# Two attentions with other bank turns, one semaphore renewal fewer, and a query stage joined to its gather, in a float32 network on one core

## The reference, cut to what matters

```python
# retention, per head of 4 (256 wide for q and k, 512 wide for v)
o = (q k^T * decay) v  (+ the same through a carried state)
o = layer_norm(o);  y = (o * silu(g)) @ w_out
# forgetting attention, per head of 16 (64 wide)
p = softmax(q k^T + cum_q - cum_k, causal);  o = p v;  y = (o * silu(g)) @ w_out
# PEER, per token: 8 heads, 16 keys of each half, 16 pairs of them
s1, s2 = q1 @ keys1.T, q2 @ keys2.T
v1, i1 = top_k(s1, 16); v2, i2 = top_k(s2, 16)
vals, c = top_k(v1[:, None] + v2[None], 16)
expert = i1[c // 16] * 128 + i2[c % 16]          # 128 experts a token
act = gelu(h @ u_tab[expert].T)
out = (softmax(vals) * act) @ v_tab[expert]
```

## Time and profile before

| | |
|---|---|
| median of 3 runs | 3270.94 us (3265.91 to 3271.77) |
| profiled execution, its own time | 3268.9 us |
| its span (first to last instruction) | 3267.0 us |
| PE busy | 2811.6 us (86%) |
| DVE busy | 1836.7 us (56%) |
| POOL busy | 1197.8 us (37%) |
| ACT busy | 884.6 us (27%) |
| gathered by POOL's queue | 536.94 MB, 40.4% of 16 DMA engines' span |

### The profile page before, as it was taken

One profiled execution on the slowest core, in us unless ns is written; L12 is line 12 of the kernel. 1 busy time (PEld: TensorE's weight loads), 2 busy tenths in 40 slices (PEclk: granted clock), 3 DMA queues, 4 the chain that ended last, 5 costly groups with the idle time before them and its releaser, 6 DMA issues. The chain is left out here.

```text
span 3267.0 us, 30767 instructions
## 1 busy us (share of the span) xinstructions
PE 2811.6 (86%) x10832; PEld 1870.9 (57%) x10832; DVE 1836.7 (56%) x3274; ACT 884.6 (27%) x1621; POOL 1197.8 (37%) x1220
## 2 busy tenths in 40 slices
PE   6999899999799989889999996778677867787777
PEld 5888477875477667689877782333233323333333
DVE  4772545333453556455624368787688568854554
ACT  2122123342345646332432331111111111111111
POOL 0000000000020414145000117777777777777774
PEclk7999999999899999999999998889798988898989
DMA  6462032310123022300222439999999999999997
GB/s 218 152 219 91 13 123 74 102 52 1 39 78 103 27 66 78 122 1 1 92 90 87 152 107 388 419 416 417 419 419 419 419 418 419 419 419 419 419 419 315
DMA packets 228769, 706.45 MB, mean 216 GB/s; under 512 B 23188, under 2 KB 25492, under 8 KB 227735
## 3 DMA queue, kind: packets, MB, share of 16 engines
q0 software_dynamic: 147456, 536.94, 40.4%
q1 hardware_dynamic: 81176, 167.76, 15.0%
HBM read 694.13 MB, written 10.49 MB: 216 GB/s over the span
## 5 line engine op out<-in xcount | busy, mean ns | idle before, releaser
L3028 PE MATMUL work_banks<-v_rows,sig 128*128 128x512 f32 x1408 | 659.5, 627 | 121.9 <-ACT sig L3019 116.3
L3028 PEld LDWEIGHTS work_banks<-v_rows,sig 128*128 128x128 f32 x1408 | 280.5, 201 | 495.7 <-issue 340.0
L219 DVE TENSOR_TENSOR weights_low<-weights_raw,weights_high 128x2048 fp32r<-128x2048 f32 x108 | 251.3, 2327 | 451.0 <-ACT weights_high L214 440.8
L3028 PE MATMUL work_banks<-weights_raw,sig 128*128 128x512 f32 x512 | 284.3, 718 | 189.4 <-ACT sig L3019 189.4
L2925 DVE CUSTOM_DVE_ANT_0 proj_banks<-u_rows,work_banks 128x1024 f32<-128x1024 f32 x256 | 314.1, 1230 | 206.7 <-DMA u_rows<-in_peer_u_dram,eidx 206.7
L277 PE MATMUL proj_banks<-h_low,weights_high 128*128 128x512 f32 x896 | 358.6, 400 | 30.4 <-DVE weights_low L219 12.9
L2700 POOL DMA_INDIRECT v_rows<-in_peer_v_dram,eidx x352 | 332.2, 944 | 115.8 <-issue 91.5
L214 ACT CAST weights_high<-weights_raw 128x2048 fp32r<-128x2048 f32 x108 | 205.9, 1906 | 617.7 <-PE proj_banks L277 600.9
L277 PE MATMUL proj_banks<-h_high,weights_high 128*128 128x512 f32 x896 | 353.1, 394 | 0.0
L277 PE MATMUL proj_banks<-h_high,weights_low 128*128 128x512 f32 x896 | 353.0, 394 | 0.0
L3028 PEld LDWEIGHTS work_banks<-weights_raw,sig 128*128 128x128 f32 x512 | 116.5, 234 | 356.1 <-issue 291.3
(11 more groups left out here) (487 smaller groups left out, 4607.1 us busy)
## 6 DMA issues: line engine op xcount, KB each, us to landing
weights_raw<-in_w_in_dram SPq DMA_DIRECT2D x36, 1024.0 KB, 5.1
weights_raw<-in_ret_w_in_dram SPq DMA_DIRECT2D x24, 1024.0 KB, 5.2
ret_gate<-in_mod_w_dram SPq DMA_DIRECT2D x20, 1024.0 KB, 8.2
weights_raw<-in_fox_w_in_dram SPq DMA_DIRECT2D x16, 1024.0 KB, 5.2
weights_raw<-in_ret_w_out_dram SPq DMA_DIRECT2D x8, 1024.0 KB, 5.0
weights_raw<-in_peer_w_q_dram SPq DMA_DIRECT2D x8, 1024.0 KB, 5.2
v_rows<-in_peer_v_dram,eidx POOLq DMA_INDIRECT x352, 16.6
ret_v<-in_mod_w_dram SPq DMA_DIRECT2D x4, 1024.0 KB, 13.3
```

What stands on the lines that cost most here:

```text
L219: nc.vector.tensor_tensor(wlo[h][:, :, :], raw[h][:, :, :], whi[h][:, :, :].bitcast(F32), ALU.subtract).then_inc(w_split[h], 1)
L3028: last = nc.tensor.matmul(pa[:, half, :], diag[:, s, e, :], v_row(s, e)[:, half * CW:(half + 1) * CW], start=(first and e == 0), stop=(las ...
```

## The change

It has four parts.

1. Retention's attention: three output banks instead of two and one for transposes. A bank is free as soon as it is normalised (`nrm_ready`), the gate product goes to POOL, `nrm` has two buffers, and a tile's transposes come three tiles after its outputs.
2. Forgetting attention: DVE multiplies the outputs of the two banks into the gate first, in turn with ACT's copies of the sums so that the two engines are never on one bank, and the reciprocal follows. values(m+1) waits for the two products and the two copies (`o_read`, `sums_ready`) alone.
3. The `recycle_semaphores()` between `delta_inputs` and `delta_rule` is left out.
4. The query stage and the gather stage become one block. The gather's buffers lie over the split weights and the input parts, now with names of their own (`over_split`, `over_parts`), and waits on `first_used` and `s_full` stand in for the barrier. Four more v rows are gathered inside the query part, 16 instead of 12. PE does scores(c-1) after two of the four tiles of a first half instead of after all four. DVE takes the first top_head of a chunk before the split of the next half chunk, and `experts(0, 0)` right after the heads 2 and 3.

```diff
-                nrm = sbuf(st2, "ret_nrm", [P, CW])
+                nrm = sbuf(st2, "ret_nrm", [P, 2, CW])
+                O_BANKS, LAG = 3, 3
...
+                        def output(n):
+                            h, t = n // TT, n % TT
+                            pe.wait_ge(s_read, n + 1)
+                            if n >= O_BANKS:
+                                pe.wait_ge(nrm_ready, n - O_BANKS + 1)
...
+                        def transposes(n):
+                            h, t = n // TT, n % TT
+                            pe.wait_ge(gated, n + 1)
+                            if n:
+                                pe.wait_ge(tr_read, n)
...
+                        for n in range(RET_HEADS * TT):
+                            if n % TT == 0 and n // TT + 1 < RET_HEADS:
+                                scores(n // TT + 1)
+                            output(n)
+                            if n >= LAG:
+                                transposes(n - LAG)
...
-                                nc.vector.tensor_tensor(sg[:, t, cols], sg[:, t, cols], nrm[:, :],
-                                                        ALU.mult).then_inc(gated, 1)
...
+                            pool.wait_ge(nrm_ready, n + 1)
+                            cols = slice(h * RET_HV, (h + 1) * RET_HV)
+                            nc.gpsimd.tensor_tensor(sg[:, t, cols], sg[:, t, cols], nrm[:, n % 2, :], ALU.mult
+                                                    ).then_inc(gated, 1)
...
                                 pe.wait_ge(o_read, m)
+                                pe.wait_ge(sums_ready, 2 * m)
...
+                            act.wait_ge(down_read, m + 1)
...
+                            nc.vector.tensor_tensor(sg[down, m, :], sg[down, m, :], pa[down, 3, :], ALU.mult
+                                                    ).then_inc(down_read, 1)
+                            dve.wait_ge(sums_ready, 2 * m + 1)
+                            nc.vector.tensor_tensor(sg[up, m, :], sg[up, m, :], pa[up, 2, :], ALU.mult
+                                                    ).then_inc(o_read, 1)
...
-                            dve.wait_ge(scaled_gate, m + 1)
-                            nc.vector.tensor_tensor(sg[up, m, :], sg[up, m, :], pa[up, 2, :], ALU.mult)
-                            nc.vector.tensor_tensor(sg[down, m, :], sg[down, m, :], pa[down, 3, :], ALU.mult
-                                                    ).then_inc(o_read, 1)
...
+            over_split = sbuf(st2, "rows_over_split", [P, GE, D], side="right")
+            over_parts = sbuf(st2, "rows_over_parts", [P, GE, D], side="right")
+            vr = sbuf(st2, "v_rows", [P, 3, D])
...
+                    sp.wait_ge(s_full, 4 * n)
...
-                        project_half(pe, c, 0, parts)
+                        project_half(pe, c, 0, parts, tiles=range(0, 2))
                         scores(c - 1)
+                        project_half(pe, c, 0, parts, tiles=range(2, 4))
                         project_half(pe, c, 1, parts)
...
+                    pool.wait_ge(first_used, state["g"] + n + 1)
+                    for e in range(GE // 2, GE):
+                        gather_row(v_row(0, e), v_tab, 0, e).then_inc(v_loaded[0][e], 16)
+                    pool.wait_ge(s_full, 4 * n)
...
-                recycle_semaphores()
                 delta_rule(qkv, sc, sig, osb)
```

More of the change, by code:

```diff
@@ L1055, in _ @@
-                        scores(0)
-                        for h in range(RET_HEADS):
-                            if h + 1 < RET_HEADS:
-                                scores(h + 1)
-                            outputs(h)
-                            transposes(h)
+                        def output(n):
[3 more added lines that the diff above has]
+                                pe.wait_ge(nrm_ready, n - O_BANKS + 1)
+                            for j in range(t + 1):
+                                last = nc.tensor.matmul(pa[:, n % O_BANKS, :], sc[:, h % 2, j, t * P:(t + 1) * P],
+                                                        v[:, j, h * RET_HV:(h + 1) * RET_HV],
+                                                        start=(j == 0), stop=(j == t))
+                            last.then_inc(o_full, 1)
@@ L1062, in _ @@
+                        scores(0)
+                        for n in range(RET_HEADS * TT):
[4 more added lines that the diff above has]
+                                transposes(n - LAG)
+                        for n in range(RET_HEADS * TT - LAG, RET_HEADS * TT):
+                            transposes(n)
                     @block.vector
@@ L2782, in _ @@
                     sp.wait_ge(x_put, 16)
+                    sp.wait_ge(s_full, 4 * n)
+                    for t in range(TT):
+                        sp.dma_start(xr[:, :], x_away[:, t, :]).then_inc(x_back[t], 16)
+                        sp.wait_ge(y_added, t + 1)
+                        sp.dma_start(out[0, t * P:(t + 1) * P, :], xr[:, :]).then_inc(out_stored[t], 16)
+                        sp.wait_ge(out_stored[t], 16)
                 @block.tensor
@@ L3020, in _ @@
                                                      scale=coef[:, g % 2, e:e + 1]).then_inc(diag_ready, 1)
-                def weigh(pe, r, s, t, first, last_of_tile):
+                @block.gpsimd
+                def _(pool):
+                    pool.wait_ge(eidx_ready, 1)
                     for e in range(GE):
-                        pe.wait_ge(diag_ready, r * (2 * GE) + (t * NG * GE + s * GE + e + 1))
-                        pe.wait_ge(v_loaded[s][e], r * 16 + 16 * (t * NG // 2 + 1))
-                        for half in range(2):
-                            last = nc.tensor.matmul(pa[:, half, :], diag[:, s, e, :],
-                                                    v_row(s, e)[:, half * CW:(half + 1) * CW],
-                                                    start=(first and e == 0),
-                                                    stop=(last_of_tile and e == GE - 1))
-                        last.then_inc(v_used, 1)
@@ new lines, in gather @@
+                    def gather(table, g, s, used, loaded, rows=(0, GE)):
+                        t, first = g // NG, (g % NG) * GE
+                        if table is u_tab and g % (NG // 2) == 0:
+                            pool.wait_ge(eidx_ready, g // (NG // 2) + 1)
+                        for e in range(*rows):
+                            pool.wait_ge(used, g * GE + (e + 1))
+                            gather_row(u_row(s, e) if table is u_tab else v_row(s, e), table, t, first + e
+                                       ).then_inc(loaded[s][e], 16)
@@ L3057, in build @@
+                    for g in range(1, LAST):
+                        gather(u_tab, g, g % 2, dot_done, u_loaded)
+                        gather(v_tab, g, g % 2, v_used, v_loaded)
+                    for rows in SEGMENTS:
+                        gather(u_tab, LAST, LAST % 2, dot_done, u_loaded, rows)
+                        gather(v_tab, LAST, LAST % 2, v_used, v_loaded, rows)
+            stage_end(n)
     then_out = columns(a["fox_w_out"][0])
```

255 lines of the change are left out of this document (108 added, 147 removed).

## The result

The changed kernel takes 3239.36 us (median of 4 runs, 3237.68 to 3243.29) where the kernel before takes 3269.82 (4 runs): ratio 0.9909, 95% interval 0.9893 to 0.9925, so 30 us faster. The forecast was 3226, with a range from 3217 to 3241. The sum said -45.0 us against one profiled execution; the profiled execution after has a span of 3238.6 us against 3267.0, which is -28.4. So 16.6 us of the forecast gain are missing, and the question is where.

A forecast was written before the change was run, and what follows sets the result against it. PE's waits and hand-overs bound it up to about 1960 us, full DMA engines in the gather behind. -13.7 - 19.5 - 0.9 - 10.9 = -45.0 us from 3268.9; with runs' median 2.0 higher, 3226 us, range 3217 to 3241.

The forecast's parts named there:

- an attention that gives less: Rival, both attentions: slow clock in the second and POOL hand-overs that show cost 10 us, giving 3236; chance 0.13.
- a joined stage that gives nothing: Rival, query stage and gather: DVE holds PE back or first groups wait for slots; 10.9 us lost, 3237; chance 0.10.
- Retention's attention: Term for the first attention: gate product on POOL, PE stops waiting for DVE; -13.7 us, between -11.7 and -16.
- Forgetting attention: Term for the second attention: PE's waits for DVE's last product go, the tail shortens; -19.5 us, between -14 and -20.
- Renewal: Term for the boundary ahead of the delta rule: less time between store's landing and next issue; -0.9 us, -0.5 to -1.2.
- Seam of query stage and gather: Term for the joined stage: earlier steady issue 5.9 us, more gathers already out 5.0; -10.9 us, between -7.6 and -11.
- Four gathers more, 4 x 1.249: Part of the joined stage's gain: sixteen gathers issued before the steady issue instead of twelve, worth 5.0 us.
- The split beside the first gathers: Query stage: DVE's split could cost one gather up to 2.3 us, hidden by POOL's idle 4 us ahead of gather 17.
- the steady rate stays, since the same 1008 gathers follow at the rate of a full DMA: Step for the long gather: its rate per gather is unchanged, so no loss enters the sum.
- 1008 at 1.25: Sign of being right, in POOL's timeline: after a gap of some 4 us, 1008 gathers at 1.25 us each.
- 1.29 and more a gather: Sign of being wrong, in the gather: each gather takes 1.29 us or more.
- the third rival: Gather runs slower from new row places or phase; sign turns from 1.294 us a gather, at 1.30 3277 us; chance 0.03.

The follow-up runs named there:

- run 7: The changed kernel with ten of its sixteen moved gather rows 224 bytes lower, at 256 modulo 512: 3223.94 us against 3267.26 for the kernel before, ratio 0.9873.
- run 10: The kernel before with the joined query and gather stage alone: 3279.59 us against 3267.38, ratio 1.0031.
- run 11: The kernel before with the joined query and gather stage alone, ten moved rows put at 256 modulo 512 bytes: 3263.84 us against 3267.38, ratio 0.9989.
- run 12: The changed kernel again, unaltered, as control: 3237.99 us against 3267.38 for the kernel before, ratio 0.9912.
- run 3: The kernel before with 32 bytes left free ahead of u_rows_first, so 23 of 32 rows lie 32 bytes off: 3422.66 us against 3421.11, ratio 1.0004.
- run 5: The changed kernel with constants moved and 32 bytes left free, so all rows begin at multiples of 64 bytes: 3382.06 us against 3422.25 for the kernel before.
- Run 4: The changed kernel with the eight rows of rows_over_parts at eight different places modulo 512 bytes: 3384.60 us, one run.
- run 2: The kernel before with both attentions' changes and the renewal left out, peer stages as before: 3382.75 us against 3421.11, ratio 0.9886.

## Why the prediction was right, and which step failed

The time lies in the range, near its upper end, and the sign is right. That it lies there is partly luck: the range was opened to 3241 for an attention that gives less or a joined stage that gives nothing, and neither came. A loss that the sum had at zero happened to fit into the same room. Point by point:

- **Retention's attention, -13.7 forecast, -15.5 in the trace, -14 as a run.** Right in mechanism and within its range. DVE is busy 36.6 us where 37.2 was said, POOL's products take 1.27 us where 1.3 was taken, and PE's waits are for ACT's copies (3.6 us) and no product.
- **Forgetting attention, -19.5 forecast, -19.8 in the trace, -19 as a run.** Pairs are 10.2 us apart, the last reciprocal follows the last values by 1.4 us with the two products ahead of it, and the granted clock is 0.99 where it was 0.91: with the waits gone it is near full, as priced.
- **Renewal, -0.9.** The load leaves 0.4 us behind the landing, as said. No run had it alone; it is under what runs can tell.
- **Seam of query stage and gather, -10.9 forecast, -9.3 by landings.** Near in sum, less so in its terms. The indices came 5.1 us earlier in their stage, not 7.5 (first gather 90.5 us behind the stage's start before, 85.4 now). The sum let the split between the two picks start at once; DVE waited 3.4 us for ACT's high part (the line is below). "Four gathers more, 4 x 1.249" counted issues where landings bind: 12 had landed in both when the steady issue began. What was gained in its place is that the queue no longer runs empty: gather 13 lands 0.5 to 1.1 us behind the time at which gather 17 is issued (here and in runs 7, 10, 11 and 12), and before 5.1 us behind its own issue. POOL's gap ahead of gather 17 was 0.94 us and not 4, since the later indices and the slow first gather used it up.
- **The split beside the first gathers.** The first took 2.94 us where 1.16 was before, the second 0.94. It was issued at 1900.63, and the split ran from 1900.25 to 1902.53: the 2 us that the prediction allowed for. The Trainium skill ("SBUF — State Buffer", Who interferes with whom) says less than the prediction took from it: that a `tensor_tensor`, which the split is, holds up GpSimd's reads, while a DMA of GpSimd was not seen to stall beside one. Here one did.
- **The failed step is "the steady rate stays, since the same 1008 gathers follow at the rate of a full DMA".** The full DMA of this kernel has no fixed rate. Its rate hangs on the places that it writes to: 1.275 us a landing before, 1.292 after, 17.7 us over the gather, and runs 7, 10 and 11 show that the places of the rows are the cause. Of its own signs, "1008 at 1.25" failed (1.271 by issues), and "1.29 and more a gather" came true by landings, not by issues. (Its 1.249 is 1264.4 us over 1012; there are 1011 steps, so 1.251.) This is the third rival, *slower*, given 0.03. Its mechanism was right, its price a third of what it said: I priced only the rate from which it turns the sign, not the smaller ones, which have more chance and cost a part of the gain. The argument against it ("the same bytes by the same queue, in the same order of tables") named everything but what the change altered.
- With that term in place the sum is -45.0 + 17.7 = -27.3, against -28.4. The rest is the attentions' and the seam's small differences, and the clock in the first and the third line of the account.

The split that waited, with the pick behind it, in the changed kernel's query stage:

```profile
1882.58 2.29 DVE L219 TENSOR_TENSOR weights_low<-weights_raw,weights_high 128x2048 fp32r<-128x2048 f32 x1 [3.38 <-ACT weights_high L214]
1884.79 0.28 DVE L2717 MAX8 peer_v<-peer_sc 128x8 f32<-128x128 f32 x1
```

The three parts as ratios, 0.9957 x 0.9938 x 1.0031 = 0.9926, stand against 0.9912 for the whole; the difference is within their intervals, and the renewal is not in the product.

## What stays open

What a fast place is. All rows at 256 modulo 512 are fast, and all others of the table slow, `x_res` at 128, a multiple of 64, among them. The Trainium skill ("DMA: Bandwidth & Descriptors", How a descriptor splits into AXI transactions) says, by the vendor's account and of what is read, that a descriptor which does not start at a multiple of 256 bytes begins with a transaction from the multiple below, whose unused bytes still cost beats. The places here are those that are written. The table agrees with 256, and so do the packets of run 3 (rows at 288) and of run 5 (128, 192, 384), though not their times, which this can't be read from on their chips. Run 4 does not quite: in its packets 64 did better than 0. The packet records tell only part: `x_res` has packets of 159 ns and yet lands every 1.27 to 1.28 us, so the slower rows may lose time between packets too. No run put a row at 0 where landings could be read. Nor was a kernel with all rows at multiples of 256 run: at its widest stage the kernel has not 32 bytes of SBUF left, so `x_res` and `weights_raw` can't be shifted by a gap of their own, and the six rows left in `rows_over_split` lie on split tiles whose neighbours are still read when the first of them are gathered.

## What to carry to other kernels

Where a transfer bounds a stage, the addresses of its buffers are part of its rate: before moving them, note each one's place modulo 512 bytes (256 is the fast one here), and compare the intervals between landings tile by tile, since a share of full engines (1.03 in all kernels on the faster chips) hides 1.2% of rate. Read a queue that runs ahead by its landings, never by its issues: issues said that four gathers were gained, landings said none. And when a rival is a rate, price it at small sizes too, not only where it turns the sign.

## What the hardware showed that was not expected

- 32 bytes of offset raised the share of packets over 160 ns from 5.6 to 43.6% (runs 2 and 3); ten rows moved by 224 bytes are worth 14 to 16 us of 3240 (runs 7 and 11).
- On two chips the same programs ran 4.2 to 4.7% longer, nearly all of it in the gather, 371 to 373 GB/s against 414 to 419, with about 3% of the packets at 200 ns and more. There the place of the rows cost nothing measurable in time, so it is worth trying a tuning of this kind on more than one chip.
- POOL stood 28 to 29 us ahead of the landings at the end of the gather without a wait of its own showing it.
